# Input pairs of a hybrid encoder block: where the gate blocks' Silu, the weight loads and the second rotated block stand in their queues

## The reference

```python
proj = x @ w_in[l]
aq, ak, av, dqkv, dbeta, da, dz, gates = jnp.split(proj, SPLIT_POINTS, axis=-1)
aq = apply_rope(aq.reshape(B, S, N_Q_HEADS, HEAD_DIM), cos, sin)
ak = apply_rope(ak.reshape(B, S, N_KV_HEADS, HEAD_DIM), cos, sin)
dqkv = jax.nn.silu(causal_depthwise_conv(dqkv, conv_w[l]))
...
o_dn = o_dn * jax.nn.silu(dz.reshape(B, S, DN_HEADS, DN_HEAD_DIM).astype(jnp.float32))
```

## Time and profile before

| | |
|---|---|
| runs of the kernel before (3) | median 1398.19 us, 1397.06 to 1398.72 |
| the profiled execution | 1397.5 us |
| its span, first to last instruction | 1395.7 us |
| mean granted TensorE clock | 0.997 |
| busy: PE, PEld, DVE, ACT, POOL | 1373.6, 1140.1, 1025.1, 607.8, 177.7 us |
| chain that ended last, by engine | PE 87%, DVE 6%, DMA 4%, SP's queue 2% |
| the input pairs on TensorE | about 33.7 to 311 us |

### The profile page before, as it was taken

One profiled execution on the slowest core, in us unless ns is written; L12 is line 12 of the kernel. 1 busy time (PEld: TensorE's weight loads), 2 busy tenths in 40 slices (PEclk: granted clock), 3 DMA queues, 4 the chain that ended last, 5 costly groups with the idle time before them and its releaser, 6 DMA issues.

```text
span 1395.7 us, 21990 instructions
## 1 busy us (share of the span) xinstructions
PE 1373.6 (98%) x8400; PEld 1140.1 (82%) x8400; DVE 1025.1 (73%) x1890; ACT 607.8 (44%) x1306; POOL 177.7 (13%) x163
## 2 busy tenths in 40 slices
PE   9999998999999999999999999999999999999997
PEld 8788887787888888788888888888888888888885
DVE  7999885855888888655358796766665777777778
ACT  4655534432344444532113455455554544444540
POOL 4322322230000000235800000000000000000002
PEclk9999999999999999999999999999999999999999
DMA  6232344675443542244612153444335875555422
GB/s 215 91 121 106 121 162 157 223 230 172 120 108 99 133 111 56 80 151 153 231 81 110 52 190 121 166 166 166 151 126 220 302 240 176 161 165 180 128 69 120
DMA packets 123497, 206.83 MB, mean 148 GB/s; under 512 B 40865, under 2 KB 61569, under 8 KB 121089
## 3 DMA queue, kind: packets, MB, share of 16 engines
q1 hardware_dynamic: 113312, 183.93, 40.1%
q10 hardware_dynamic: 10080, 21.50, 4.1%
HBM read 142.92 MB, written 62.47 MB: 147 GB/s over the span
## 4 chain that ended last, share of the span: by engine, by line
PE 87%; DVE 6%; DMA 4%; SPq 2%; issue 1%; ACT 0%; ACTq 0%; POOL 0%; DVEq 0%; POOLq 0%
PE ps L2590 6%; PE ps L2588 6%; PE ps L2589 6%; PE ps L2209 6%; PE ps L2571 6%; PE ps L2572 6%; PE ps L2573 6%; PE ps L2157 5%; PE ps L2158 5%; PE ps L2159 5%; PE ps L2275 4%; PE ps L2096 4%; PE ps L2097 4%; PE ps L2095 4%; PE ps L2465 2%; PE ps L2469 2%
## 5 line engine op out<-in xcount | busy, mean ns | idle before, releaser
L2588 PE MATMUL ps<-thi,shi 128*128 128x512 f32 x416 | 161.8, 389 | 0.0
L2589 PE MATMUL ps<-tlow,shi 128*128 128x512 f32 x416 | 161.8, 389 | 0.0
L2590 PE MATMUL ps<-thi,slow 128*128 128x512 f32 x416 | 161.8, 389 | 0.0
L943 ACT ACTIVATE thi<-b 128x512 fp32r<-128x512 f32 x104 | 65.5, 630 | 108.0 <-PE ps L2590 108.0
L1979 DVE TENSOR_TENSOR tlow<-b,thi 128x512 fp32r<-128x512 f32 x104 | 71.8, 690 | 52.7 <-ACT thi L943 52.6
L2589 PEld LDWEIGHTS ps<-tlow,shi 128*128 128x128 f32 x416 | 78.1, 188 | 16.3
L933 POOL TENSOR_TENSOR zt<-zt,ln2gb 128x256 f32<-128x256 f32 x4 | 3.4, 852 | 690.7 <-ACT zt L1394 690.7
L2590 PEld LDWEIGHTS ps<-thi,slow 128*128 128x128 f32 x416 | 78.1, 188 | 16.2
L2588 PEld LDWEIGHTS ps<-thi,shi 128*128 128x128 f32 x416 | 78.1, 188 | 16.0
L1972 DVE TENSOR_TENSOR slow<-sraw,shi 128x512 fp32r<-128x512 f32 x104 | 71.3, 686 | 21.7 <-ACT shi L943 20.6
L943 ACT ACTIVATE shi<-sraw 128x512 fp32r<-128x512 f32 x104 | 65.1, 626 | 31.6 <-DMA zt<-xpark 16.4
(11 more groups left out here) (445 smaller groups left out, 3827.5 us busy)
## 6 DMA issues: line engine op xcount, KB each, us to landing
raw<-in_wblk SPq DMA_DIRECT2D x55, 512.0 KB, 4.5
sraw<-hpark SPq DMA_DIRECT2D x104, 256.0 KB, 2.8
hpark<-hq SPq DMA_DIRECT2D x16, 1024.0 KB, 4.9
b<-in_wblk SPq DMA_DIRECT2D x64, 256.0 KB, 3.5
wraw<-in_wblk SPq DMA_DIRECT2D x30, 512.0 KB, 4.0
hpark<-hq SPq DMA_DIRECT2D x16, 768.0 KB, 4.9
park<-cb ACTq DMA_DIRECT2D x34, 256.0 KB, 3.9
park<-cacc ACTq DMA_DIRECT2D x12, 512.0 KB, 3.2
```

The lines of the kernel that those rows point to most:

```text
L943: cp = lambda o_, i_: act.activation(o_, i_, ACT.Copy)
L2588: mm(outp, shi[s][:, ts], thi[m][:, :], start=first, stop=False, skip_group_check=True)
L2589: mm(outp, shi[s][:, ts], tlow[m][:, :], start=False, stop=False, skip_group_check=True)
L2590: return mm(outp, slow[s][:, ts], thi[m][:, :], start=False, stop=final, skip_group_check=True)
```

## The change

In SP's loop the second half block of an iteration is no longer loaded at the end of that iteration but in the next one, behind the next weight loads, and stored there before the next first half block is loaded. The iteration ends with the store of the first half block. VectorE rotates the second half block one iteration later, behind the low parts A11, A22 and A12 and ahead of `combine_in(n, 0)`. In ScalarE's iterations 9 and 10 `store_pair` (with its two Silu and four DMA issues) stands behind snapshot 2 instead of behind snapshot 1. The number of instructions stays as it is.

```diff
-                before, (first, second) = ROPE_AT.get(n - 2, (None, None))[1], ROPE_AT.get(n - 1, (None, None))
+                before, first = ROPE_AT.get(n - 2, (None, None))[1], ROPE_AT.get(n - 1, (None, None))[0]
+                if before is not None:
+                    rope_load(before)
+                if n > DEC0 + 1:
+                    dec_load(2 * (n - DEC0) - 1)
                 if before is not None:
                     rope_store(before)
                 if first is not None:
                     rope_load(first)
-                if n > DEC0 + 1:
-                    dec_load(2 * (n - DEC0) - 1)
+                if n > DEC0:
+                    dec_load(2 * (n - DEC0))
                 if first is not None:
                     rope_store(first)
-                if n > DEC0:
-                    dec_load(2 * (n - DEC0))
-                if second is not None:
-                    rope_load(second)
...
                 in_snap(n, 1)
-                if n > N_DN // 2:
+                if n > N_DN // 2 and not B_DZ < 2 * n < B_GATE + 1:
                     store_pair(n - 1)
...
                 in_snap(n, 2)
+                if n > N_DN // 2 and B_DZ < 2 * n < B_GATE + 1:
+                    store_pair(n - 1)
...
                     decay_rates()
+                if ROPE_AT.get(n - 1, (None, None))[1] is not None:
+                    rope(ROPE_AT[n - 1][1])
                 combine_in(n, 0)
...
                 in_lo(n + 1, "S3")
-                if ROPE_AT.get(n, (None, None))[1] is not None:
-                    rope(ROPE_AT[n][1])
```

## The result

| | before | after |
|---|---|---|
| runs side by side | 1397.62 us median of 4 (1396.81 to 1398.72) | 1407.37 us median of 4 (1406.19 to 1408.74) |
| ratio, 95% interval | | 1.0070 (1.0052 to 1.0087) |
| the profiled execution, its span | 1397.5, 1395.7 us | 1408.3, 1406.5 us |
| mean granted TensorE clock | 0.997 | 0.994 |

What follows compares the result with a forecast made beforehand. TensorE, 98% busy, waits in the input pairs for weights held by SP's one-buffer loop of rotated blocks. Start 235.4 plus rounds 23.7 and 22.8 put pair 12's S4 6.0 us later: 1404.2 us, range 1395.4 to 1410.5.

Steps and rivals of the forecast that it cites:

- Part 1: ScalarE, iterations 9 and 10: Silu behind the third snapshot removes gaps before S3 of pairs 9 and 10; 2.9 us gained.
- case 5: Silu move does nothing because S1's sum comes late: 2 us less gain, absorbed; 0.60 together with the forecast's own side.
- Part 2: SP's order and VectorE's late rotation: rounds of 23.7 and 22.8 us against TensorE's 19.04; pair 12's S4 6.0 us later.
- (a): SP's loop, from issue of a pair's weights to the end of A12's low part: taken 10.1 us.
- (b): SP's loop, VectorE rotates the second half block, partly beside GpSimd's sums: taken 2.3 us.
- (c): SP's loop, store of the second half block until the next load: taken 2.0 us.
- (d): SP's loop, load of the first half block to its rotation: taken 6.0 us, 6.9 with a table.
- (e): SP's loop, rotate the first half block, 2.0 us, and issue its store, 0.4 us.
- W(11): Time at which SP issues pair 11's weights (W(n): pair n's); forecast 235.4, where it was 234.77.
- Case 1: Faster: SP's loop does not bind and the gaps close; 1391.1 us with all, 1394.8 with lowest rows; chance 0.14.
- Case 2: Within 0.2%: a round of 21 us makes pair 12's S4 0.5 us later, 1398.7 us; chance 0.21.
- Case 4: Over 11 us slower, steps towards upper ends; decay exponentials and snapshots wait behind the first half block's rotation; chance 0.05.

Runs made afterwards that it cites:

- order alone: Changed kernel with the Silu move taken back, SP's and VectorE's new order kept: 1405.16 us, 1.0056 of the kernel before.
- again: The changed kernel run once more, nothing edited: 1406.44 us, 1.0062 of the kernel before.
- sums first: Changed kernel with the decay sums ahead of rotation 1 in VectorE's iteration 8: 1404.36 us, 1.0054 of the kernel before.
- weights and table ahead: Kernel before with Silu move, earlier store 2 and load 3, second decay load behind weights, rotation table and weights loaded still earlier: 1397.90 us, 1.0003.
- weights ahead: Changed kernel with the next pair's weight loads ahead of the first half block's store from SP's iteration 10 on: 1402.26 us, 1.0041 of the kernel before.
- hoist alone: Kernel before with block 2's store and block 3's load ahead of SP's decay loads in iteration 10, Silu unmoved: 1395.52 us, 0.9982.
- load 8 first: Changed kernel with loads of half blocks 8 and 9 ahead of the decay load that waits for an exponential's store: 1402.18 us, 1.0027.

## Why the prediction was right, and where its sizes were off

**What bounds, and Part 1.** The reading of the gaps held: pair 9's gap went with the Silu, so case 5 falls. In the changed kernel the Silu stood at 225.39 and not at 220.6: pair 9 began 2.2 us late, so that the third snapshot came at 223.48, and a table load of 1.28 us stands between that snapshot and the Silu. "The gain of 2.1 in pair 9 is waited away" holds in the changed kernel and not by itself: alone the move gained 3.2 us. I had costed the Silu and the snapshots behind it but not the four stores of `store_pair`, which stand beside block 3's load in the kernel before and, as that load comes later, beside it in the changed kernel again.

**Part 2, the round.** That the new order makes SP's loop longer than a pair is shown: the order alone is slower by 6.9 us, its rounds last 22.75 and 21.01 us, those of the changed kernel 24.27 and 22.98 (again: 24.21 and 22.23), and a start 5.5 us earlier leaves them at 22.84 and 23.02. That this loop makes the whole loss, as the forecast had it, is not so: the pairs hold 7.15 and 3.8 us of it in the two executions of the changed kernel, and 2.9 in order alone. By steps, in the first execution, first and second round: (a) 10.08 and 10.21 against 10.1; (b) 3.14 and 3.13 against 2.3; (c) 2.62 and 3.25 against 2.0; (d) 5.93 with the table and 3.90 against 6.9 and 6.0; (e) 2.50 and 2.49 against 2.4. The sums came within 0.6 us since (b) and (c) were too small and (d) too large: a right sum with wrong terms. For (b) these rows of VectorE and GpSimd show why:

```profile
244.40 1.78 DVE L1480 TENSOR_TENSOR ipA12l<-raw,ipA12h 128x512 fp32r<-128x512 f32 x1
246.11 1.78 DVE L1557 TENSOR_TENSOR rraw<-rraw,rtab 128x512 f32<-128x512 f32 x1
...
245.71 1.63 POOL L885 TENSOR_TENSOR s4raw<-raw,ipS2r 128x512 f32<-128x512 f32 x1
```

GpSimd's sum at 245.71 to 247.34 held rotation A's first instruction at 1.78 us, where the earlier trace rows have 0.69; the same at 270.51. I had taken "partly beside the sums", 0.3 us of such a hold; in both rounds it was a whole one, 1.1 us. By the rule of the Trainium skill that the prediction named, SBUF — State Buffer, section Who interferes with whom, step (b) would have stood at its upper end of 3.1 us. The trace agrees (3.14 and 3.13), and for this step that was the better estimate.

**The start.** Decay sums to 210.55 against 209.3, the gap at pair 9's start 1.92 against 0.8: rotation 1 began at 205.66, behind the upper end of 205.5, and one of its instructions took 1.78. Pair 10's weights, said to come 1.7 us earlier, were issued at 209.23, where they were at 209.13. W(11) = 236.03 against 235.4. "Absorbed" was the expectation for this gap too; the run with the sums first speaks against it (2.1 us between the medians, not clear of the noise).

**The end of the pairs.** Pair 12's S4 stood at 290.86 against 289.8, 7.1 us later than before instead of 6.0; the pairs ended 7.2 us later. To here the sum holds within 1.2 us in this execution. In the second one S4 stood at 287.03, 2.8 us ahead of the forecast: the sum sits between the two.

**The clock.** The prediction said what one more low clock behind pair 12's gap would add: 1.6 us. There was none. The stretches are those of pair 9's start, of the gaps before S2 and S4 of pair 11, and of the gaps before S2 and S4 of pair 12 (columns as in the earlier trace rows):

```profile
210.00:216.00 6.00, 5.31 (x16) 4.28 (x17) 3.57 (x8) 1.49 (x5) 0.00 (x0) 0.72 0.58 200
...
262.00:270.00 8.00, 5.67 (x18) 4.31 (x19) 6.94 (x11) 4.25 (x9) 2.87 (x2) 0.79 0.92 310
286.00:294.00 8.00, 6.11 (x26) 4.80 (x27) 7.71 (x11) 5.07 (x10) 4.67 (x3) 1.00 0.73 255
```

The first two low stretches lie ahead of later waits for weights, which hide them in part. The one behind the wait for tb has no such wait behind it.

**The step that failed** is the last one, "SP reaches the scan's first loads near 312 instead of 303, their data is there near 320, and they are needed near 323: no cost". SP reached them at 316.98, and the cost was 3.6 us. Two things were missed. From W(14) to the scan's loads SP took 16.65 us instead of 12.08, as blocks 8 and 9 wait behind a decay load which waits for an exponential. And the price is not that these data come late: it is that their transfer runs beside the stores for which ScalarE waits. That the loads were needed late enough was true and was the wrong question. Moving block 8's load alone brought the wait back to 2.27 (1.7 us less) but not the clock, and the median fell by 4 to 5 us. Had this term been in the sum, 1404.2 would have been 1407.8. That this lies so close to the measured 1407.37 is in part luck: the pairs took 1.2 us more than the sum had, the profiled execution lay 0.9 above the median where it had been 0.7 below, and in the second execution the scan's term is 5.6 us and the pairs' 3.8.

**The rivals.** Case 1, the loop doesn't bind, falls with the rounds. Case 2 needed rounds of 21 us; only the second rounds of order alone and sums first, 21.01 and 21.33, come near, and the time rules it out. Case 4's chain, the exponentials behind rotation B, exists and makes gaps of 2.74 and 1.30, which S4's wait absorbs in part; taken by itself it is worth the most once the weights are out of the way (4.99).

## What to carry to other kernels

When a queue serves a chain through one buffer (load, work, store, load), write the chain down as a loop from one event back to itself, with the instructions that now stand ahead of each step on every engine, and compare its length with the time of the bottleneck engine. If it is longer, everything gained before it is at risk, and each stage adds its difference. Then follow the same queue past the stage's end: what it issues there late can collide with transfers that somebody waits for, though its own data are in time. And moving a block of instructions moves its transfers: price these against the loads on whose landing the loop stands.

## What the runs showed of the hardware

- A store of a half block took 2.0 us from its issue to the dependent load's issue with quiet queues, 2.6 and 3.3 in the two rounds of the changed kernel, and 5.5 right behind the issue of 1 MB of weights (weights and table ahead). Some 3 us behind such an issue it was 3.7 there and 2.0 to 2.6 in weights ahead.
- The granted clock behind the wait of 2.2 to 2.3 us for tb was 1.00 in the kernel before and in four others, and low in three (hoist alone, load 8 first, weights ahead: 0.66 to 0.75 over five or six us); the scan's stretch was then 276.6 to 276.7 us instead of 275.1 to 275.2. A gap of one length thus came with 1.5 us more or without; which, the gap alone doesn't say.
- Two executions of the changed kernel had W(11) at 236.03 and 233.39 and the pairs at 262.9 and 259.6 us, while their spans differ by 1.7. By these two, terms of one execution are good to some 3 us here, and their sum to less.
